# First weight block behind a norm, computed chunk by chunk of 128 tokens, in a two-layer hybrid decoder trunk

## Chip, cores and metric

The kernel runs on all 8 cores of one Trainium2 chip. Each core works on one of the 8 sequences of the batch, with no traffic between cores. The metric is the device time of the slowest core in microseconds (us).

## What is computed

Per core x is 4096 tokens by 1024 channels. Three matrix-heavy parts follow each other per layer, each behind an RMSNorm of the residual stream h; the weights are bf16 on the chip, sums are in f32.

```
for layer in (0, 1):
    y = rmsnorm(h, norm_mix_g[layer])
    if layer == 0:
        u, v, z, xBC, dt = split(y @ w_in)                  # 1024 -> 5136
        a = gelu(u) * (W_s layernorm(gelu(v)) + b)          # gMLP gating, chunks of 128
        b = rmsnorm(ssd(silu(conv(xBC)), dt) * silu(z))     # Mamba-2 scan, chunks of 128
        h = h + [a | b] @ w_out
    else:
        q, k, v = split(y @ w_qkv + b_qkv)                  # 16 heads, 2 kv heads
        h = h + window_attention(q, k, v, sinks) @ w_o + b_o
    y = rmsnorm(h, norm_mlp_g[layer])
    h = h + square(relu(y @ w_up[layer])) @ w_down[layer]   # 1024 -> 4096 -> 1024
out = rmsnorm(h, final_norm_g)
```

## The kernel before

A core takes its sequence in 8 tiles t = 0..7 of 512 tokens. A tile is 4 chunks of 128 tokens, since a norm needs tokens on the 128 partitions. `rmsnorm` (the function that yields once per chunk) does for each chunk: an ACT Square with accumulated sum (`yb<-h`), two POOL instructions for the inverse root (`small`), a DVE scalar_tensor_tensor that writes the normalized bf16 chunk (`yb<-h,small,rowb`, line 777), 8 transposes on PE (`ps<-ident_bf,yb`, line 827) into one PSUM bank, and a copy on DVE or ACT of that bank into the columns of the chunk in yTA, yTB or yT2 (`yTA<-ps`), which hold the tile with channels on partitions. From tile 4 on, the norms of rows 0, 2 and 4 (ahead of the input projection, the attention and the second MLP) transpose with a DMA and use neither PE nor PSUM; row 1 (ahead of the first MLP, called norm1) always uses PE.

The weights are cut into 51 blocks of 1024 by 512. A block lies in one of the four ring buffers `wring` and is computed by four calls of `fmajor`. Each call takes one PSUM bank and runs 8 matmuls of 512 columns into it, with 128 output channels of the block as weights and all 512 tokens of the tile as the moving side. So the first matmul of a block waits for all four chunks of the norm. Each bank is then emptied by ACT, in the MLP by a relu of 128x512 (`scr<-ps`, line 747), which DVE squares (`scr<-scr`, line 759).

PSUM has 8 banks in two pools of four, poolA and poolB, handed out in turn. The two streams that run side by side, for instance the attention of one tile and the output projection of another, have a pool each. A norm and the block behind it use the same pool.

The code only records operations with their reads and writes. A planner (`schedule`, with five passes over the recorded program, in which due times are worked out from the end) then sets one fixed order for each engine, by list scheduling over its own estimates of durations; semaphore waits are put in where an operation depends on another engine. PE works in that order: a matmul that waits holds up all that stand behind it. The reads and writes of PSUM are tracked by bank, so two matmul groups in one bank, or a group and the transposes that used the bank before, stay in the recorded order.

The record goes through the stages of the two streams with `zip_stages`. Tiles 0 and 1 go together through the first MLPs (`ups`, `dns`); from tile 2 on `mlp` does a tile at a time.

Of the kernel before, what the change touches and what calls it, by code (L numbers as in the profile page):

```python
# [8 lines left out]
AF = mybir.ActivationFunctionType  # L9
# [471 lines left out]
def _isap(x):  # L481
    return hasattr(x, "tensor") and hasattr(x, "ap")
# [3 lines left out]
PP_BQ = 80  # L486
# [20 lines left out]
PACE = 24  # L507
PST = 2
PASSES = 6
GATES = [(("w0", 0), ("x", 0, 1)), (("w0", 1), ("x", 0, 1)), (("w", 1), ("x", 1, 0)), (("w", 2), ("x", 1, 1)), (("w", 3), ("x", 1, 2)),  # L510
         *[(("x", 1, c), ("w0", 0)) for c in range(4)],
         (("gm", 0), ("w", 2)), (("gm", 1), ("w", 2)), (("ac", 0, 0), ("w", 2)), (("ac", 0, 1), ("w", 2)),
# [4 lines left out]
def build(NT=8):  # L517
    slots = due = None
    for n in range(PASSES):
        nc, st, P = record(NT, slots)  # L520
        P.due = due
        if n + 1 < PASSES:
            P.schedule()
            if n == PASSES - 3:
                due = P.backward()
            if n != PASSES - 3:
                slots = P.reslot(NW)
# [4 lines left out]
def record(NT, slots):  # L532
    nc = bass.Bass("TRN2", target_bir_lowering=False)
    st = ExitStack()
    P = Prog()
# [125 lines left out]
    qT = sview(AT, [8, 512], BF16)  # L661
# [35 lines left out]
    def nfree(ap):  # L697
        n = 1
        for s in ap.shape[1:]:
            n *= s  # L700
        return n

    def c_act(ap, accum=False):
        return 0.066 + nfree(ap) * 0.000833 + (0.12 if accum else 0.0)
# [27 lines left out]
    def ACT(out, in_, func, bias=None, scale=None, accum=None):  # L732
        kw = {}
        rd = [in_]
        wr = [out]
        if bias is not None:
            kw["bias"] = bias
            if _isap(bias):
                rd.append(bias)
        if scale is not None:  # L740
            kw["scale"] = scale
            if _isap(scale):
                rd.append(scale)
        if accum is not None:
            kw["accum_out"] = accum
            wr.append(accum)
        P.op("act", lambda e: e.activation(out=out, in_=in_, func=func, **kw), reads=rd, writes=wr,  # L747
             dur=c_act(in_, accum is not None) + 0.083 * (_isap(bias) + _isap(scale)), single=True,
             tset=TSETS.get(func))
# [39 lines left out]
    def PE(mms, extra_reads=(), writes=None):  # L789
        rd = list(extra_reads)  # L790
        wr = []
        d_ = 0.0
        l0 = mms[0][1]
        mode = 1 if l0.shape[0] == 64 else 2 if nfree(l0) == 64 else 0
        for (o, l, r, s0, s1) in mms:
            rd.append(l)
            rd.append(r)
            wr.append(o)
            d_ += c_mm(r, l)
        if writes is not None:  # L800
            wr = writes

        def fn(e, w=None):
            ins = None
            for n_, (o, l, r, s0, s1) in enumerate(mms):
                ins = e.matmul(o, lhsT=l, rhs=r, start=s0, stop=s1)  # L806
                if n_ == 0 and w is not None:
                    ins._wait_ge(w[0], w[1])
            return ins
        P.op("pe", fn, reads=rd, writes=wr, dur=d_, single="first", mode=mode)  # L810
# [44 lines left out]
    ppc = lambda c: pp[:, c:c + 1]  # L855
# [28 lines left out]
    last = NT - 1  # L884

    def wget(t, bb):
        slot = ws["free"].pop(0) if slots is None else slots[len(P.blks)][0]
        kc, cols = blocks[bb]
        n = kc * cols
        dst = wring[slot][:, 0:n]  # L890
        blk = Blk(slot)
        P.blks.append(blk)
        P.fills = blk
        store = False
        if bb not in ws["seen"]:
            nse = len(ws["seen"])
            ws["seen"].add(bb)
            if nse == 0:
                P.fills = None
                for q in range(2):  # L900
                    part = slice(q * n // 2, (q + 1) * n // 2)
                    DMA(dst[:, part], wpk_d[bb, :, part], ch_w0[q], eng="pool", issue=0.65)
                    P.mark["w0", q] = len(P.recs) - 1
                    P.early[len(P.recs) - 1] = 1e8 - 1e5 * q
                    blk.w.append(len(P.recs) - 1)
            else:
                DMA(dst, wpk_d[bb, :, 0:n], ch_ring_sw[slot], eng="pool", issue=0.65)
                if nse < 4:
                    P.early[len(P.recs) - 1] = 1e8 - 1e6 * nse
            P.mark["w", nse] = len(P.recs) - 1  # L910
            if B_WOUT <= bb < B_WOUT + 4 and (bb - B_WOUT) % 2 == 1:
                dv = dst.rearrange("p (k c) -> p k c", c=cols)
                for q in range(8):
                    TS("dve", dv[:, q, :], dv[:, q, :], ppc(PP_NG + q), ALU.mult)
            store = t < last
        else:
            DMA(dst, wscr[bb, :, 0:n], ch_ring[slot])
        P.fills = None
        if store:
            P.touch.add(blk)  # L920
            DMA(wscr[bb, :, 0:n], dst, ch_wst[slot])
            P.mark["s", len(ws["seen"]) - 1] = len(P.recs) - 1
        return Wt(P, blk, dst.rearrange("p (k c) -> p k c", c=cols))
# [73 lines left out]
    def fmajor(wv, o, yT, pool):  # L997
        bk = pool.next()
        MMG(bk, [(wv[:, k, o * 128:(o + 1) * 128], yT[:, k, :]) for k in range(8)])
        return bk  # L1000

    def tmajor(wv, tc, yT, pool):
        bk = pool.next()
        MMG(bk, [(yT[:, k, tc * 128:(tc + 1) * 128], wv[:, k, :]) for k in range(8)])
        return bk
# [115 lines left out]
            yield from z_blk(t, B, pool, wv, bi, True)  # L1121

    def u_blk(t, wv, bi, pool, fin=False):
        for o in range(4):
            P.tag = "u"
            bk = fmajor(wv, o, yd(t), pool)
            ACT(bufs(t).guT[:, 4 * bi + o, :], bk, AF.Gelu_apprx_tanh)
            if fin and o == 3:
                wdone(wv)
            yield  # L1130
# [147 lines left out]
    def ups(l, ts, fh, hp, pools):  # L1278
        yTs = [yTA, yTB]
        for b in range(0, 4, 2):  # L1280
            wvs = [wget(0, (B_UP1 if l else B_UP0) + 4 * fh + b + i) for i in range(2)]
            for t in ts:
                for i, wv in enumerate(wvs):
                    for o in range(4):
                        P.tag = "mlp%d" % l
                        bk = fmajor(wv, o, yTs[t], pools[t])
                        r = r32[o % 2]
                        ACT(r, bk, AF.Relu)
                        TT("dve", hp[:, t, 4 * (b + i) + o, :], r, r, ALU.mult)
                        if t == ts[-1] and o == 3:  # L1290
                            wdone(wv)
                        yield
# [18 lines left out]
    def mlp(t, l, yT, pool, mid=None):  # L1311
        h = hs_[t % 2]
        P.tag = "mlp%d" % l
        bu = B_UP0 if l == 0 else B_UP1
        bd = B_DN0 if l == 0 else B_DN1
        for f in range(32):
            if f % 4 == 0:
                wv = wget(t, bu + f // 4)
            bk = fmajor(wv, f % 4, yT, pool)
            r = r32[f % 2]  # L1320
            ACT(r, bk, AF.Relu)
            TT("dve", hid[:, f, :], r, r, ALU.mult)
            if f % 4 == 3:
                wdone(wv)
            yield
        yield from accum_out(t, bd, 4, lambda k: hid[:, k, :], h, pool, mid)
# [53 lines left out]

    def qkv(t, yT, pool):
        wv = wget(t, B_QKV)
        for o in range(4):
            ACT(qT[:, o, :], fmajor(wv, o, yT, pool), AF.Identity, bias=ppc(PP_BQ + o))
            yield
        wdone(wv)
        wv = wget(t, B_QKV + 2)
        bkk = fmajor(wv, 0, yT, pool)
        for kv in range(2):
            p_ = slice(64 * kv, 64 * kv + 64)  # L1390
            o_ = slice(64 - 64 * kv, 128 - 64 * kv)
            ACT(kT[p_, kv, 128:640], bkk[p_, :], AF.Identity, bias=ppc(PP_BK)[p_, :])
            DMA(kT[o_, kv, 128:640], kT[p_, kv, 128:640], ch_kt[kv])
        yield
        bk = pool.next()
        PE([(bk[:, tc * 128:(tc + 1) * 128], yT[:, k, tc * 128:(tc + 1) * 128], wv[:, k, 128:256], k == 0, k == 7)
            for tc in range(4) for k in range(8)], writes=[bk])
        TT("dve", vtok[:, 1:5, :], bk.rearrange("p (c d) -> p c d", d=128),
           bcv(BC_BV, 128).unsqueeze(1).to_broadcast([128, 4, 128]), ALU.add)
        wdone(wv)  # L1400
        yield
# [94 lines left out]
    yd = lambda t: yTB if t == 1 else yT2 if t == 2 else yTA  # L1496
# [103 lines left out]

    for a, b in GATES:
        P.recs[P.mark[a]][2].add(P.mark[b])
# [82 lines left out]
```

How the kernel before makes its waits and increments, by code:

```python
            def body(eng):  # L453
                for i in order[ename]:
                    e_, fn, deps, chan, dur, xfer = recs[i]
                    wl = list(fw[i])
                    fused = wl.pop() if (wl and self.single[i] and self.FUSE_WAIT) else None
                    for k, v in wl:
                        eng.wait_ge(sems[k], v)
                    if fused is not None and self.single[i] == "first":
                        ins = fn(eng, (sems[fused[0]], fused[1]))
                    else:
                        ins = fn(eng)
                        if fused is not None:
                            ins._wait_ge(sems[fused[0]], fused[1])
                    if chan is not None:
                        ins.then_inc(sems[chan.key], 16)
                    else:
                        ins.then_inc(sems[ename], 1)
                if ename == "sp":
                    for k, v in finals.items():
                        eng.wait_ge(sems[k], v)
# [330 lines left out]
        def fn(e, w=None):  # L803
            ins = None
            for n_, (o, l, r, s0, s1) in enumerate(mms):
                ins = e.matmul(o, lhsT=l, rhs=r, start=s0, stop=s1)
                if n_ == 0 and w is not None:
                    ins._wait_ge(w[0], w[1])
            return ins
# [14 lines left out]
        def fn(e, w=None):  # L824
# [2 lines left out]
                ins = e.transpose(out=o, in_=i_, identity=idn)  # L827
                if n_ == 0 and w is not None:
                    ins._wait_ge(w[0], w[1])
            return ins
```

The softmax here doesn't subtract the row's maximum and nothing guards it: scores larger than these inputs give would overflow.

## Time and profile before

| | |
|---|---|
| median of 3 runs | 3198.69 us (3195.86 to 3713.0) |
| profiled execution, its own time | 3202.78 us |
| its slowest core, first to last instruction | 3201.2 us (the 8 cores: 3187.0 to 3201.2) |
| PE busy | 3091.2 us, 97% of the span, 16400 matmuls |
| DVE / ACT / POOL busy | 57% / 47% / 16% |
| granted TensorE clock, mean of that core | 0.986 |

The profile is of the slowest core, number 6. Busy time counts instructions from start to end; matmuls overlap in the array, so that a busy PE is one that has a matmul under way. Idle time of an engine stands in brackets or behind a bar, with the instruction of another engine that ended it. A granted clock of 1.00 is 2.4 GHz, one of 0.5 is 1.2 GHz.

### The profile page before, as it was taken

The page shows a single profiled execution, that of the slowest core. Times are in us where ns is not written, and L with a number is a line of the kernel's source. Part 1 is how long each engine was busy: PE and PEld are TensorE (multiplying, and loading weights), DVE is VectorE, ACT ScalarE, POOL GpSimd, SP SyncE. Part 2 cuts the span into 40 slices and gives each one's busy share as a digit, 9 for nine tenths or more (in the row PEclk, how much of TensorE's full clock was granted, in tenths as well). Part 3 has the DMA queues.
Part 4 walks back from the last instruction along what each step waited for, and adds up shares of the span by engine and source line. Part 5 has one row for each costly group of instructions (what it writes and reads, how often), then busy time and mean ns, then how long its engine had stood idle before and what let it go on. Part 6 is the DMA issues. An engine that isn't in the chain of part 4 may idle for free.

```text
span 3201.2 us, 40536 instructions; the slowest of 8 cores (3187.0 to 3201.2 us)
## 1 busy us (share of the span) xinstructions
PE 3091.2 (97%) x16400; PEld 1443.9 (45%) x16400; DVE 1819.2 (57%) x2409; ACT 1497.2 (47%) x2473; POOL 503.1 (16%) x857
## 2 busy tenths in 40 slices
PE   8897999989999999999999999999999999999999
PEld 4344444434444444444544444444444444444444
DVE  5788334665454765537754486636846187454532
ACT  7775213694243644427543273624736166342421
POOL 3332101121012121001210122102210022100000
PEclk9998999999999999999999999999999999999999
DMA  9678778557757385444874469554794648637553
GB/s 201 158 161 221 167 182 203 148 157 185 178 167 228 120 251 177 147 164 139 232 236 152 145 202 235 197 165 151 222 245 153 184 145 237 211 131 201 158 182 127
DMA packets 197757, 581.42 MB, mean 182 GB/s; under 512 B 113857, under 2 KB 116673, under 8 KB 143938
## 3 DMA queue, kind: packets, MB, share of 16 engines
q1 hardware_dynamic: 190082, 525.87, 53.1%
q0 software_dynamic: 7488, 52.96, 10.5%
q8 instruction: 129, 2.11, 0.3%
q14 instruction: 58, 0.48, 0.1%
HBM read 535.00 MB, written 69.99 MB: 189 GB/s over the span
## 4 chain that ended last, share of the span: by engine, by line
PE 81%; DVE 6%; ACT 5%; DMA 5%; POOL 2%; issue 1%; SPq 0%; POOLq 0%; ACTq 0%; DVEq 0%
PE ps L806 80%; ACT scr L747 3%; DVE scr L759 3%; DMA scr<-acT 2%; DVE scr L777 1%; POOL small L759 1%; DMA wring<-wpk 1%; PE ps L827 1%; DMA h<-x 1%; ACT L747 1%; ACT yb L747 1%; POOL small L766 1%; DMA yTA<-acT 1%; DVE yb L777 1%; DVE h L759 0%
## 5 line engine op out<-in xcount | busy, mean ns | idle before, releaser
L806 PE MATMUL ps<-wring,scr 128*128 128x512 bf16 x5760 | 1275.4, 380 | 6.6 <-DVE h L759 2.2
L747 ACT ACTIVATE scr<-ps 128x512 f32<-128x512 f32 (+4 forms) x988 | 631.1, 658 | 755.0 <-PE ps L806 675.4
L806 PEld LDWEIGHTS ps<-wring,scr 128*128 128x128 bf16 x5760 | 560.5, 98 | 673.8 <-issue 18.1
L806 PE MATMUL ps<-yTA,wring 128*128 128x512 bf16 x3344 | 757.5, 381 | 3.1 <-ACT scr L747 1.8
L759 DVE TENSOR_TENSOR scr<-scr 128x512 bf16<-128x512 f32 (+2 forms) x648 | 465.7, 728 | 299.4 <-ACT scr L747 290.3
L806 PE MATMUL ps<-yTB,wring 128*128 128x512 bf16 x2672 | 615.8, 383 | 5.6 <-ACT scr L747 3.6
L759 DVE TENSOR_TENSOR h<-ps,h 128x512 f32<-128x512 f32 x288 | 197.8, 689 | 584.5 <-PE ps L806 564.4
L806 PEld LDWEIGHTS ps<-yTA,wring 128*128 128x128 bf16 x3344 | 320.9, 98 | 402.8 <-issue 32.5
L806 PEld LDWEIGHTS ps<-yTB,wring 128*128 128x128 bf16 x2672 | 259.6, 99 | 316.8 <-issue 18.0
L747 ACT ACTIVATE scr<-scr 128x256 bf16<-128x256 f32 (+4 forms) x442 | 272.1, 622 | 171.1 <-DVE scr L759 144.8
L747 ACT ACTIVATE yb<-h 128x1024 bf16<-128x1024 f32 x120 | 126.3, 1053 | 419.2 <-DVE h L759 396.0
L777 DVE SCALAR_TENSOR_TENSOR scr<-scr,pp_sb 128x512 f32<-128x512 f32 x384 | 280.0, 748 | 67.7 <-ACT scr L747 62.8
L766 POOL TENSOR_SCALAR small<-small 128x1 f32<-128x1 f32 (+1 forms) x224 | 85.0, 379 | 1425.2 <-ACT yb L747 867.5
L747 ACT ACTIVATE scr<-ps,pp_sb 128x512 f32<-128x512 f32 (+1 forms) x192 | 142.9, 747 | 123.2 <-PE ps L806 120.4
L806 PE MATMUL ps<-wring,yTA 128*128 128x512 bf16 (+1 forms) x832 | 176.7, 369 | 1.8 <-DMA wring<-wpk 0.9
L759 POOL TENSOR_TENSOR small<-small,mhalf 128x1 f32<-128x1 f32 (+1 forms) x224 | 164.4, 734 | 18.2
L747 ACT ACT_TABLE_LOAD x116 | 148.8, 1283 | 6.7 <-DVE h L768 2.6
L806 PEld LDWEIGHTS ps<-wring,yTA 128*128 128x128 bf16 x832 | 78.7, 98 | 92.8 <-issue 1.7
L759 DVE TENSOR_TENSOR scr<-scr,mask 128x1024 bf16<-128x1024 bf16 x126 | 86.4, 689 | 39.4 <-ACT scr L747 38.1
L759 DVE TENSOR_TENSOR scr<-ps,scr 128x512 bf16<-128x512 f32 (+1 forms) x96 | 82.8, 864 | 31.4 <-ACT scr L747 16.8
L759 DVE TENSOR_TENSOR scr<-scr,dts 128x1024 f32<-128x1024 f32 (+1 forms) x74 | 91.5, 1244 | 14.8 <-POOL scr L1184 9.3
L777 DVE SCALAR_TENSOR_TENSOR yb<-h,small,rowb 128x1024 bf16<-128x1024 f32 x60 | 76.9, 1282 | 38.3 <-POOL small L759 38.2
(122 smaller groups left out, 1832.2 us busy)
## 6 DMA issues: line engine op xcount, KB each, us to landing
wring<-wscr SPq DMA_DIRECT2D x320, 1024.0 KB, 5.9
wscr<-wring SPq DMA_DIRECT2D x50, 1024.0 KB, 10.5
wring<-wpk POOLq DMA_DIRECT2D x49, 1024.0 KB, 11.6
scr<-acT SPq DMA_DIRECT2D x42, 512.0 KB, 8.8
h<-x SPq DMA_DIRECT2D x36, 512.0 KB, 8.5
out<-scr SPq DMA_DIRECT2D x32, 512.0 KB, 8.2
rowb<-rows SPq DMA_DIRECT2D x28, 512.0 KB, 5.8
scr<-x SPq DMA_DIRECT2D x24, 512.0 KB, 6.6
```

The costliest lines, as they stand in the source:

```text
L747: P.op("act", lambda e: e.activation(out=out, in_=in_, func=func, **kw), reads=rd, writes=wr, dur=c_act(in_, accum is not None) + 0.083 * ...
L759: P.op(eng, lambda e: e.tensor_tensor(out=out, in0=in0, in1=in1, op=op), reads=[in0, in1], writes=[out], dur=(0.57 if nfree(out) < 16 else ...
L766: P.op(eng, lambda e: e.tensor_scalar(out=out, in0=in0, scalar1=s1, scalar2=None, op0=op0), reads=rd, writes=[out], dur=d_, single=True)
L777: P.op("dve", lambda e: e.scalar_tensor_tensor(out=out, in0=in0, scalar=scalar, in1=in1, op0=op0, op1=op1), reads=rd, writes=[out], dur=c_ ...
L806: ins = e.matmul(o, lhsT=l, rhs=r, start=s0, stop=s1)
L827: ins = e.transpose(out=o, in_=i_, identity=idn)
```

## The change

A new function `by_chunk` takes the four PSUM banks of the pool at once. It runs the same block as 16 groups of 8 matmuls of 128 columns: for each chunk c, for each quarter o of the block's output channels, the 8 matmuls of (c, o) into columns c*128 to c*128+127 of bank o. A group reads the columns of its own chunk alone. The four banks are emptied as before, each by one instruction of 512 columns, behind the group of the last chunk. It is used for 21 blocks: the first up block of both MLPs for every tile (16 blocks), the first Q block where the norm stands directly ahead of it (tiles 0, 1, 2 and 7), and the first u block of tile 3. All other blocks keep `fmajor`.

```diff
+BYC = 31
...
+    def by_chunk(wv, yT, pool):
+        bks = [pool.next() for _ in range(4)]
+        for c in range(4):
+            cs = slice(c * 128, (c + 1) * 128)
+            for o in range(4):
+                PE([(bks[o][:, cs], wv[:, k, o * 128:(o + 1) * 128], yT[:, k, cs], k == 0, k == 7) for k in range(8)],
+                   writes=[bks[o]])
+        return bks
...
     def u_blk(t, wv, bi, pool, fin=False):
+        P.tag = "u"
+        bks = by_chunk(wv, yd(t), pool) if BYC & 16 and t == 3 and bi == 0 else None
         for o in range(4):
             P.tag = "u"
-            bk = fmajor(wv, o, yd(t), pool)
+            bk = bks[o] if bks else fmajor(wv, o, yd(t), pool)
...
+                    bks = by_chunk(wv, yTs[t], pools[t]) if BYC & 8 and fh == 0 and b == 0 and i == 0 else None
...
+            if f == 0 and BYC & (1 << l):
+                bks = by_chunk(wv, yT, pool)
+            bk = bks[f] if f < 4 and BYC & (1 << l) else fmajor(wv, f % 4, yT, pool)
...
+        bks = by_chunk(wv, yT, pool) if BYC & 4 and (t <= 2 or t == last) else None
         for o in range(4):
-            ACT(qT[:, o, :], fmajor(wv, o, yT, pool), AF.Identity, bias=ppc(PP_BQ + o))
+            ACT(qT[:, o, :], bks[o] if bks else fmajor(wv, o, yT, pool), AF.Identity, bias=ppc(PP_BQ + o))
```

The planner runs on the new record, so the order of all five engines changes, also in places where the code is the same.

The order of PE at norm1 of tile 1, ahead of its first MLP. `wring,scr` are matmuls of the output projection, `ident_bf,yb` the transposes of one chunk, `yTB,wring` the up blocks; ps0 and ps1 are two banks each. Before:

```order
L806 MATMUL ps1<-wring2,scr 128x512 x8
L827 MATMUL ps0<-ident_bf,yb1 128x128 x8
L806 MATMUL ps1<-wring2,scr 128x512 x8
L827 MATMUL ps0<-ident_bf,yb0 128x128 x8
L827 MATMUL ps1<-ident_bf,yb1 128x128 x8
L827 MATMUL ps1<-ident_bf,yb0 128x128 x8
L806 MATMUL ps0<-yTB,wring1 128x512 x16
L806 MATMUL ps1<-yTB,wring1 128x512 x16
```

and with the change:

```order
L807 MATMUL ps1<-wring2,scr 128x512 x8
L828 MATMUL ps0<-ident_bf,yb1 128x128 x8
L807 MATMUL ps1<-wring2,scr 128x512 x8
L828 MATMUL ps0<-ident_bf,yb0 128x128 x8
L807 MATMUL ps0<-yTB,wring1 128x128 x32
L828 MATMUL ps1<-ident_bf,yb1 128x128 x8
L828 MATMUL ps1<-ident_bf,yb0 128x128 x8
L807 MATMUL ps1<-yTB,wring1 128x128 x24
L807 MATMUL ps0<-yTB,wring1 128x128 x16
```

Four of the 16 groups have moved between the transposes of the second and the third chunk; the other 12 stand behind those of the fourth.

The order of PE at the input norm of tile 3, ahead of its u block (`yTA,wring`), with the output projection of tile 2 beside it (`wring,scr`). Before:

```order
L827 MATMUL ps1<-ident_bf,yb0 128x128 x8
L806 MATMUL ps2<-wring3,scr 128x512 x16
L806 MATMUL ps3<-wring3,scr 128x512 x16
L806 MATMUL ps2<-wring2,scr 128x512 x16
L827 MATMUL ps1<-ident_bf,yb1 128x128 x8
L806 MATMUL ps3<-wring2,scr 128x512 x16
L827 MATMUL ps0<-ident_bf,yb0 128x128 x8
L806 MATMUL ps1<-yTA,wring0 128x512 x8
```

and with the change:

```order
L807 MATMUL ps3<-wring3,scr 128x512 x16
L807 MATMUL ps1<-yTA,wring1 128x128 x8
L807 MATMUL ps0<-yTA,wring1 128x128 x8
L807 MATMUL ps1<-yTA,wring1 128x128 x8
L807 MATMUL ps0<-yTA,wring1 128x128 x8
L807 MATMUL ps2<-wring0,scr 128x512 x16
L828 MATMUL ps1<-ident_bf,yb1 128x128 x8
L807 MATMUL ps3<-wring0,scr 128x512 x8
L807 MATMUL ps1<-yTA,wring1 128x128 x8
L828 MATMUL ps0<-ident_bf,yb0 128x128 x8
L807 MATMUL ps1<-yTA,wring1 128x128 x8
L807 MATMUL ps3<-wring0,scr 128x512 x8
```

Here four groups stand ahead of the third chunk's transposes and a fifth ahead of the fourth's, and 8 matmuls of the output projection have moved behind the fourth's.

## Rows read from the trace of the kernel before

**Rows 1.** The page: span; busy time, share and instructions of each engine.
```profile
span 3201.2 us, 40536 instructions; the slowest of 8 cores (3187.0 to 3201.2 us)
PE 3091.2 (97%) x16400; PEld 1443.9 (45%) x16400; DVE 1819.2 (57%) x2409; ACT 1497.2 (47%) x2473; POOL 503.1 (16%) x857
```

**Rows 2.** Waits of PE, whole span: total us, times, longest us.
```profile
PE ps L827 <- DVE yb L777: 27.7, 16, 5.9
PE ps L806 <- ACT scr L747: 21.7, 22, 3.1
PE ps L806 <- DVE scr L759: 20.1, 15, 4.6
PE ps L827 <- ACT scr L747: 10.9, 5, 6.4
PE ps L806 <- DMA wring<-wpk: 0.9, 1, 0.9
```

**Rows 3.** Windows view, nine norms: length, busy of five engines, clock, DMA.
```profile
255.00:278.00 23.00, 12.78 (x109) 8.96 (x110) 20.89 (x25) 12.55 (x24) 8.43 (x12) 0.68 0.99 214
342.00:358.00 16.00, 11.94 (x62) 5.86 (x61) 6.69 (x9) 7.31 (x13) 3.96 (x10) 0.79 0.31 106
990.00:1005.00 15.00, 10.46 (x41) 4.35 (x40) 4.54 (x4) 3.93 (x6) 0.79 (x2) 0.77 0.94 287
1036.00:1050.00 14.00, 10.83 (x69) 5.60 (x68) 13.28 (x20) 3.85 (x7) 2.46 (x5) 0.76 0.32 110
1248.00:1260.00 12.00, 9.77 (x63) 4.89 (x61) 7.88 (x11) 9.58 (x15) 4.26 (x7) 0.72 0.88 272
1638.00:1647.00 9.00, 5.93 (x35) 3.03 (x36) 8.04 (x12) 8.02 (x13) 3.83 (x6) 0.81 0.97 296
2028.00:2033.00 5.00, 3.71 (x30) 1.85 (x29) 3.98 (x6) 4.74 (x7) 1.22 (x2) 1.00 0.63 227
2401.00:2408.00 7.00, 3.89 (x40) 2.02 (x38) 5.83 (x9) 6.86 (x12) 3.58 (x6) 1.00 0.63 245
2779.00:2787.00 8.00, 4.63 (x46) 2.52 (x44) 6.96 (x10) 6.59 (x9) 2.74 (x4) 1.00 0.65 256
sum 109.00, PE 73.94 PEld 39.08 DVE 78.10 ACT 63.43 POOL 31.25; mean PE 8.22 PEld 4.34 DVE 8.68 ACT 7.05 POOL 3.47
```

**Rows 4.** Timeline at norm1 of tile 1: start, us, instruction, idle before.
```profile
343.02 1.06 ACT L747 ACTIVATE yb<-h 128x1024 bf16<-128x1024 f32 x1 [0.45 <-DVE h L759]
344.90 1.03 PE L827 MATMUL ps<-ident_bf,yb 128*128 128x128 bf16 x8 [2.26 <-DVE yb L777]
...
346.95 1.03 PE L827 MATMUL ps<-ident_bf,yb 128*128 128x128 bf16 x8 [1.02 <-DVE yb L777]
...
348.77 7.41 PE L806 MATMUL ps<-yTB,wring 128*128 128x512 bf16 x27 [0.79 <-DVE yTB L755]
```

**Rows 5.** Timeline of PE: runs of 128-column and of 512-column matmuls.
```profile
988.86 0.61 PE L827 MATMUL ps<-ident_bf,yb 128*128 128x128 bf16 x8
1247.41 1.95 PE L806 MATMUL ps<-wring,yTB 128*128 128x128 bf16 x32
1059.95 1.89 PE L806 MATMUL ps<-yTB,wring 128*128 128x512 bf16 x8
1787.18 13.98 PE L806 MATMUL ps<-yTA,wring 128*128 128x512 bf16 x64
```

**Rows 6.** Groups by line and form: the weight loads of the largest group.
```profile
L806 PEld LDWEIGHTS ps<-wring,scr 128*128 128x128 bf16 x5760 | 560.5, 98 | 673.8 <-issue 18.1 <-DVE h L759 3.4 <-DVE scr L759 1.6
```

**Rows 7.** Timeline: one bank of an up block emptied by ACT, squared by DVE.
```profile
352.12 0.60 ACT L747 ACTIVATE scr<-ps 128x512 f32<-128x512 f32 x1 [2.95 <-PE ps L806]
352.75 0.69 DVE L759 TENSOR_TENSOR scr<-scr 128x512 bf16<-128x512 f32 x1 [4.04 <-ACT scr L747]
```

**Rows 8.** Windows view: the first stages, where the code is unchanged.
```profile
60.00:255.00 195.00, 167.33 (x977) 83.38 (x974) 158.00 (x225) 142.87 (x239) 71.43 (x110) 0.95 0.73 168
```

More of the change, by code:

```diff
@@ L1283, in ups @@
                 for i, wv in enumerate(wvs):
+                    P.tag = "mlp%d" % l
+                    bks = by_chunk(wv, yTs[t], pools[t]) if BYC & 8 and fh == 0 and b == 0 and i == 0 else None
                     for o in range(4):
                         P.tag = "mlp%d" % l
-                        bk = fmajor(wv, o, yTs[t], pools[t])
+                        bk = bks[o] if bks else fmajor(wv, o, yTs[t], pools[t])
                         r = r32[o % 2]
@@ L1318, in mlp @@
                 wv = wget(t, bu + f // 4)
-            bk = fmajor(wv, f % 4, yT, pool)
+            if f == 0 and BYC & (1 << l):
+                bks = by_chunk(wv, yT, pool)
+            bk = bks[f] if f < 4 and BYC & (1 << l) else fmajor(wv, f % 4, yT, pool)
             r = r32[f % 2]
```

## The prediction

> **What bounds the kernel now.** I read the page first, then the waits of PE, then the stretches around the norms, then single instructions. The page says that PE has a matmul under way in 3091.2 of 3201.2 us [rows 1]; the other engines are at 57% and less. So the kernel is bound by PE nearly everywhere, and what a change can win is the 110 us in which PE is idle, and what the clock loses beside that. What it costs is any PE time that it adds. The waits of PE [rows 2] say where the idle time lies: the largest entry, 27.7 us in 16 waits, is PE in front of the transposes of a chunk that DVE has not yet normalized. That is the place of this change. The next three (21.7, 20.1 and 10.9 us) are mostly inside the scan, the attention and the setup, where the code stays as it is.
>
> The windows view [rows 3] takes the nine norms around which PE is idle for over a microsecond: norm1 of tiles 0 to 7 (at 255, 342, 1036, 1248, 1638, 2028, 2401 and 2779 us) and the input norm of tile 3 (990). Length minus PE busy is 10.2, 4.1, 4.5, 3.2, 2.2, 3.1, 1.3, 3.1 and 3.4 us, 35.1 in all (109.00 - 73.94). In the first six the granted clock is below 1. Length times (1 - clock) is the array time lost there: 7.4, 3.4, 3.5, 3.4, 3.4 and 1.7 us; of this a part lies in the idle time.
>
> What one such place looks like is in the timeline of tile 1 [rows 4]. The transposes of chunk 3 wait 2.26 us, those of chunk 4 another 1.02, and then the first up block waits 0.79 for the last copy. The transposes then take 1.03 us for 8, against 0.61 elsewhere [rows 5]: PE runs at the lower of its two levels, 1.2 GHz, after these gaps. All this time two of the four chunks lie ready in yTB and no matmul may use them.
>
> **The change, part by part.**
>
> *More matmuls.* 21 blocks of 32 matmuls of 512 columns become 21 blocks of 128 matmuls of 128 columns, 2016 more matmuls and weight loads. The pace of either comes from two runs of different length [rows 5]: 512 columns, (13.98 - 1.89) / 56 = 0.2159 us; 128 columns with new weights for each, (1.95 - 0.61) / 24 = 0.0558 us. A block goes from 32 x 0.2159 = 6.91 us to 128 x 0.0558 = 7.14 us, 0.23 us more, and 21 of them cost 4.8 us. All of it is on the path. The run of 32 is the longest of its kind in the trace, so the price of a run of 128 is bounded: below by the same columns at the 512 pace, 0.2159 / 4 = 0.054 us, which makes the cost 0; above by a weight load of 98 ns [rows 6] that overlaps nothing, 2688 x 0.098 - 21 x 6.91 = 118 us. I take 4.8, since the run of 32 is the same instruction shape.
>
> *Groups that fill the gaps.* A group (8 matmuls, one chunk and one bank) takes 8 x 0.0558 = 0.446 us. Norm and block use the same pool of four banks, and the transposes of chunk c went through the bank of output quarter c. So group (c, o) can run only when the copies of chunks c and o are both done: 1 group after the first chunk, 4 after the second, 9 after the third. The planner's order uses less than that. Ahead of the fourth chunk's transposes stand, in the nine places in order of time, 4, 4, 5 (input norm of tile 3), 4, 7, 4, 3, 4 and 4 groups. The smaller of these times 0.446 and the idle time is 1.8, 1.8, 2.2, 1.8, 2.2, 1.8, 1.3, 1.8 and 1.8, 16.5 us. Behind the fourth transposes the five groups of the first three chunks, 2.2 us, cover the last copy: 0.79 us in tile 1 [rows 4], and as much (it stands inside the 4.5) at the input norm of tile 3. Together 18.1 us. In the other 12 blocks PE has matmuls of the other stream between the chunks, or runs on through the block; there I count nothing gained, and the 0.23 us is paid all the same.
>
> *The clock.* If a gap is broken up, PE may stay at 2.4 GHz. In places 2 to 6 the loss is 3.4 + 3.5 + 3.4 + 3.4 + 1.7 = 15.4 us; between nothing and all of it I take half, 7.7 us, since about half of the idle time in these places remains. In place 1 (tile 0), where 10.2 us are idle and DVE is busy for 20.89 of 23 us, I count nothing: its chunks are late because DVE is full, not because PE waits.
>
> *Emptying four banks at once.* In `fmajor` a bank is complete every 1.73 us, ACT needs 0.60 us and DVE 0.69 [rows 7]. In `by_chunk` the four banks are complete in the last 1.8 us of the block, the first of them 1.34 us before the next block wants it. ACT's 0.60 leaves a slack of 0.74 us, less than one 1.06 us Square of a norm [rows 4]. Behind a block that waits here stands the rest of the up blocks, and beside the attention also its score matmuls. Bounds: 0, or 21 x 1.06 = 22 us. I take one block in five that meets such an instruction, 21 x 0.2 = 4.2 us, since ACT is busy 47% of the time overall and the planner places its work around this.
>
> *The moved order.* A weight block is wanted some 5 us earlier and held as much longer. PE waited 0.9 us in all for weights [rows 2], and the ring holds four blocks of 7 us each; cost 0 as long as that lead holds. The instructions of ACT, DVE and POOL and the DMAs are the same in number; SP's and POOL's queues only see them in another order. Between 60 and 255 us, ahead of the first block that changes, PE is idle for 195 - 167.3 = 27.7 us [rows 8], in waits of the setup and the first scans, and the planner has turned that order over. It can come out either way: 0, with 8 us on both sides (some 30% of that idle time).
>
> *Sum.* -18.1 - 7.7 + 4.8 + 4.2 = -16.8 us. On the profiled execution's own 3202.78 us that is 3186.0; the median of the runs is 4.1 us lower, so I predict **3182 us**.
>
> **Rivals.**
>
> *All gaps close.* The clock stays up in all places, also for half of tile 0's 7.4 us, and the banks cost nothing: -18.1 - 15.4 - 3.7 + 4.8 = -32.4, 3166 us. For it: the gaps left are short. Against it: the fill covers only half of the 35.1 us. 15%.
>
> *The gain is taken back.* The groups wait for copies that come late in their turn, PE being in order: half of the fill is lost (9 us left), the clock still falls, the banks cost 4.2 and the new order of the first scans 8: -9 + 4.8 + 4.2 + 8 = +8, 3207 us; between this and the forecast lies everything that is partly so. For it: chunk times are set by ACT, POOL and DVE (8.04 and 8.02 of 9 us busy at 1638, rows 3), which no group makes faster, and half of PE's waits are outside the norms [rows 2]. Against it: the work put in the gaps does not have to be done later. 30%.
>
> *The weight loads bind.* Each 128-column matmul brings its own weights. If a run of 128 can't keep the pace of a run of 32, and loads come at their full 98 ns [rows 6], the 21 blocks cost 118 us in place of 4.8: 3198.7 - 16.8 + 113 = 3295 us, slower by 3%. It decides from a pace of 0.0558 + 16.8 / 2688 = 0.062 us on: beyond that the change loses. Against it: the run of 32 and the transposes hold 0.056 us [rows 5], so loads of 98 ns do overlap with other loads or matmuls. 5%. The Trainium skill speaks for a milder form of it: "TensorE: Matmul & The Clock Gate", section "Back-to-back issue gap", puts a sustained stream of weight load and matmul of 128 columns at about 81 ns each. By it the 21 blocks would cost 72.6 us, and the time would be an estimated 3250 us. The trace does not agree with it for runs of 32; no run here shows one of 128.
>
> *The change does not do what it says.* If the planner put every group behind the last chunk, only its costs would be left, 3198.7 + 9 = 3208 us. It does so in 11 of the 21 blocks; in the nine places it does not, by the order. So this is part of the second rival and has no chance of its own.
>
> **How the numbers follow.** Forecast 48% (some 3172 to 3192), all gaps close 15%, taken back 30%, weight loads 5%, and 2% for what I have not seen. The range goes from 3162 (the first rival, with 4 us of luck in the order) to 3207 (the second). About one case in five lies outside, above it more than below. A measurement of this kernel tells some 2%, 64 us, from no change: faster than 3134.7 would need more than all the idle time at norms and all the clock; 1%. Slower than 3262.7 is the weight-load case with a pace above 0.085 us, or something unseen; 4%. So 95% within 2%.
>
> **What would show it.** In the profile after: runs of 128-column matmuls on `yTA,wring` and `yTB,wring` at 0.056 us each (a run of 128 lasting 7.2 us); PE's wait for `DVE yb L777` down from 27.7 to some 10 to 15 us; the clock at 1.00 in at least half of places 2 to 6; total PE idle near 90 us. A pace of 0.08, or a PE wait for `ACT scr` that grows by more than 5 us behind the new blocks, would make it wrong; so would new idle time in the first 255 us.

## The result, and the profile after

The changed kernel takes 3168.18 us (median of 4 runs, 3161.62 to 3283.05) against 3197.28 us of the kernel before (4 runs beside it). The ratio is 0.9907, with a 95% interval of 0.9882 to 0.9932: 0.93% less, some 29 us. Ratios, here and below, leave out executions in which one die ran at a lower clock than the other; medians do not. The time is inside the range given (3162 to 3207) and 14 us under the forecast, outside of the 3172 to 3192 that the forecast stands for and nearest to the first rival (3166).

The profiled execution took 3167.08 us. Its page, the span and the busy line; all line numbers behind the new function are one higher than before:

```profile
span 3165.5 us, 44543 instructions; the slowest of 8 cores (3151.6 to 3165.5 us)
PE 3082.5 (97%) x18416; PEld 1524.8 (48%) x18416; DVE 1815.3 (57%) x2409; ACT 1497.8 (47%) x2471; POOL 502.0 (16%) x857
```

Beside [rows 1] the span is 35.7 us shorter, while PE is busy for only 8.7 us less, with 2016 matmuls more. So 27.0 us are idle time that is gone (110.0 to 83.0). The waits of PE say which (total us, times, longest):

```profile
PE ps L807 <- ACT scr L748: 17.3, 18, 2.5
PE ps L828 <- DVE yb L778: 13.7, 12, 3.6
PE ps L828 <- ACT scr L748: 12.1, 4, 5.4
PE ps L807 <- DVE scr L760: 11.2, 15, 2.3
```

The wait for a normalized chunk, 27.7 us in [rows 2], is half; the waits for ACT and DVE in front of other matmuls went down too (21.7 to 17.3 and 20.1 to 11.2), and none of size has come in their place.

The windows view of the nine norms, in order of time. These stretches run from the transposes of the first chunk to the end of the first block, so they are longer than those of [rows 3]. The columns are length, busy time of PE, weight loads, DVE, ACT and POOL, then granted clock, DMA share and GB/s:

```profile
252.30:285.50 33.20, 21.46 (x269) 19.20 (x270) 27.69 (x30) 17.44 (x33) 10.27 (x16) 0.69 1.00 227
338.00:351.00 13.00, 11.09 (x169) 9.64 (x167) 6.53 (x8) 7.57 (x13) 3.78 (x9) 1.00 0.44 158
968.00:993.50 25.50, 25.22 (x237) 16.13 (x235) 10.29 (x11) 6.53 (x9) 4.05 (x7) 1.00 0.88 308
1019.00:1033.00 14.00, 12.82 (x191) 10.96 (x190) 12.90 (x21) 4.84 (x7) 2.78 (x6) 1.00 0.40 147
1228.80:1246.80 18.00, 17.73 (x229) 13.13 (x227) 11.57 (x17) 14.65 (x22) 3.48 (x8) 1.00 0.70 289
1614.00:1631.00 17.00, 17.00 (x203) 11.95 (x202) 13.62 (x21) 13.79 (x23) 4.21 (x8) 1.00 0.61 206
1994.00:2013.00 19.00, 19.00 (x213) 12.91 (x211) 14.45 (x20) 14.53 (x24) 4.38 (x8) 1.00 0.55 168
2370.00:2389.00 19.00, 19.00 (x212) 12.94 (x211) 13.93 (x19) 14.35 (x24) 3.31 (x8) 1.00 0.64 197
2743.00:2761.00 18.00, 17.09 (x225) 13.02 (x224) 12.50 (x17) 11.87 (x17) 1.84 (x5) 1.00 0.32 119
sum 176.70, PE 160.41 PEld 119.89 DVE 123.48 ACT 105.56 POOL 38.12; mean PE 17.82 PEld 13.32 DVE 13.72 ACT 11.73 POOL 4.24
```

Eight of nine are at a clock of 1.00, where five of them were below it; three have no idle time left. The first, tile 0, is the exception: 11.7 us idle and a clock of 0.69.

To make this a sum I divide the span of the slowest core in three: idle time of PE, half of PE's busy time at the 1.2 GHz level (what that level costs), and the rest, which is work at full clock.

| us, before → after | idle | cost of 1.2 GHz |
|---|---|---|
| norm1 of tile 0 | 10.2 → 11.7 | 2.0 → 6.0 |
| norm1 of tile 1 | 4.1 → 1.9 | 2.5 → 0 |
| input norm of tile 3 | 4.5 → 0.3 | 3.0 → 0 |
| norm1 of tile 2 | 3.2 → 1.2 | 3.1 → 0 |
| norm1 of tile 3 | 2.2 → 0.3 | 3.0 → 0 |
| norm1 of tile 4 | 3.4 → 0 | 1.6 → 0 |
| norm1 of tiles 5, 6, 7 | 7.8 → 0.9 | 0 → 0 |
| the nine places | 35.3 → 16.2 | 15.2 → 6.0 |
| everywhere else | 74.7 → 66.8 | 18.7 → 13.8 |

Work at full clock went from 3057.3 to 3062.7. So: -19.1 - 9.2 (nine places) - 7.9 - 4.9 (elsewhere) + 5.4 = -35.7 us.

At norm1 of tile 1 the timeline of PE (start, us, instruction, idle before) now reads as follows; the last run also holds the blocks behind the first:

```profile
340.28 0.61 PE L828 MATMUL ps<-ident_bf,yb 128*128 128x128 bf16 x8
341.82 1.96 PE L807 MATMUL ps<-yTB,wring 128*128 128x128 bf16 x32 [0.94 <-DVE yTB L756]
343.62 0.61 PE L828 MATMUL ps<-ident_bf,yb 128*128 128x128 bf16 x8
345.20 0.62 PE L828 MATMUL ps<-ident_bf,yb 128*128 128x128 bf16 x8 [0.97 <-DVE yb L778]
345.66 14.65 PE L807 MATMUL ps<-yTB,wring 128*128 128x128 bf16 x138
```

In [rows 4] PE stood 2.26, 1.02 and 0.79 us and then transposed at 1.03 us for 8. Now 32 narrow matmuls lie between the second and the third chunk, two gaps under 1 us are left, and the transposes take 0.61 and 0.62.

### The profile page after: what moved, and what is told of

Its sections match the earlier page's. It is cut to its first block, busy times and chain, and to the rows that moved or that the text cites. A ratio compares the mean times of both kernels' runs of the same rounds, so it can differ in the third digit from the quotient of the medians.

```text
span 3165.5 us, 44543 instructions; the slowest of 8 cores (3151.6 to 3165.5 us)
## 1 busy us (share of the span) xinstructions
PE 3082.5 (97%) x18416; PEld 1524.8 (48%) x18416; DVE 1815.3 (57%) x2409; ACT 1497.8 (47%) x2471; POOL 502.0 (16%) x857
## 4 chain that ended last, share of the span: by engine, by line
PE 80%; ACT 7%; DVE 6%; DMA 5%; POOL 2%; issue 1%; SPq 0%; POOLq 0%; ACTq 0%; DVEq 0%
PE ps L807 79%; ACT scr L748 4%; DVE scr L760 3%; DMA scr<-acT 3%; ACT L748 1%; PE ps L828 1%; DMA wring<-wpk 1%; POOL small L760 1%; DVE scr L778 1%; DMA h<-x 1%; POOL small L767 0%; ACT yb L748 0%; DVE yb L778 0%; DMA scr<-scr 0%; DVE h L760 0%
## 5 line engine op out<-in xcount | busy, mean ns | idle before, releaser
L748 ACT ACTIVATE scr<-ps 128x512 f32<-128x512 f32 (+5 forms) x988 | 628.8, 659 | 782.9 <-PE ps L807 651.7
L807 PEld LDWEIGHTS ps<-wring,scr 128*128 128x128 bf16 x5760 | 559.3, 98 | 667.0 <-issue 12.4
L807 PE MATMUL ps<-yTA,wring 128*128 128x512 bf16 (+1 forms) x4400 | 764.1, 329 | 3.5 <-ACT h L748 2.2
L807 PE MATMUL ps<-yTB,wring 128*128 128x512 bf16 (+1 forms) x3632 | 609.7, 323 | 7.9 <-ACT scr L748 5.4
L807 PEld LDWEIGHTS ps<-yTA,wring 128*128 128x128 bf16 x4400 | 368.2, 98 | 366.1 <-issue 32.7
L807 PEld LDWEIGHTS ps<-yTB,wring 128*128 128x128 bf16 x3632 | 299.5, 98 | 279.1 <-issue 6.9
L807 PEld LDWEIGHTS ps<-wring,yTA 128*128 128x128 bf16 x832 | 78.7, 98 | 93.4 <-issue 1.7
L760 DVE TENSOR_TENSOR scr<-scr,dts 128x1024 bf16<-128x1024 bf16 (+1 forms) x74 | 93.0, 1263 | 33.6 <-POOL scr L1196 23.6
## 6 DMA issues: line engine op xcount, KB each, us to landing
wring<-wpk POOLq DMA_DIRECT2D x49, 1024.0 KB, 11.7
```

The costliest lines, as they stand in the source:

```text
L760: P.op(eng, lambda e: e.tensor_tensor(out=out, in0=in0, in1=in1, op=op), reads=[in0, in1], writes=[out], dur=(0.57 if nfree(out) < 16 else ...
```

## Experiments

Theory A is the prediction's: groups that start before the last chunk fill the gaps, and that keeps the clock up. Theory B: the gain comes from something else that the change brings, above all the order that the planner turned over. The table holds all runs. "Ratio" is to the kernel before on the same chip; the last two columns are idle time plus cost of 1.2 GHz, as above, on the slowest core of the profiled execution (on core 5 for whole_tile_reordered and norm_in_one_bank, whose slowest cores carry the effect told in the last section, and on core 2 for without_mlp0 and core 6 for after_third_order, since some matmul records of their slowest cores are missing).

| kernel | median us | ratio [95%] | nine places | elsewhere |
|---|---|---|---|---|
| before | 3197.28 | 1 | 35.3 + 15.2 | 74.7 + 18.7 |
| before_reordered | 3202.06 | 1.0027 [1.0008, 1.0047] | 43.1 + 15.2 | 64.7 + 18.8 |
| before_third_order | 3193.44 | 1.0000 [0.9989, 1.0010] | 34.0 + 11.4 | 70.7 + 14.7 |
| whole_tile | 3183.41 | 0.9960 [0.9947, 0.9973] | 31.1 + 15.5 | 64.3 + 9.2 |
| whole_tile_reordered | 3203.04 | 1.0005 [0.9985, 1.0025] | 32.2 + 12.1 | 64.8 + 12.8 |
| changed kernel | 3168.18 | 0.9907 [0.9882, 0.9932] | 16.2 + 6.0 | 66.8 + 13.8 |
| after_reordered | 3166.97 | 0.9907 [0.9891, 0.9923] | 15.1 + 4.7 | 66.9 + 14.4 |
| after_third_order | 3160.81 | 0.9900 [0.9885, 0.9914] | 17.2 + 3.4 | 62.0 + 11.3 |
| all_up_by_chunk | 3189.11 | 0.9969 [0.9948, 0.9990] | 17.4 + 8.1 | 64.1 + 12.4 |
| norm_in_one_bank | 3180.68 | 0.9929 [0.9902, 0.9955] | 16.8 + 4.4 | 72.3 + 18.5 |
| mlp0_only | 3175.68 | 0.9942 [0.9924, 0.9959] | 21.7 + 6.7 | 70.0 + 14.3 |
| without_mlp0 | 3180.10 | 0.9937 [0.9911, 0.9963] | 26.9 + 9.7 | 64.5 + 10.7 |
| without_late_blocks | 3168.67 | 0.9918 [0.9904, 0.9932] | 17.4 + 4.0 | 72.1 + 12.8 |
| without_late_blocks_2 | 3175.54 | 0.9939 [0.9925, 0.9953] | 15.4 + 6.1 | 74.4 + 19.7 |

**whole_tile.** The same narrow matmuls, but every group waits for all four chunks:

```diff
-                   writes=[bks[o]])
+                   extra_reads=[yT[:]], writes=[bks[o]])
```

> The change with its 16 groups per block, but every group also waits for all four chunks of its tile: the 128-column shape and a new order stay, the early start is gone. Theory A (the gain is work moved into the gaps of the norms, and the clock that this keeps up): idle time of PE at the nine norms back to about 35 us, the 1.2 GHz stretches back, 5 us more for the shape: 3195 to 3210 us. Theory B (the planner's new order makes the gain, the early start is beside the point): 3160 to 3180 us, as the order here differs from that of before in as many rows as the change's does.

It took 3183.41 us, which neither theory had. Eight of the nine norms did what A says: at norm1 of tile 1 the timeline of PE is [rows 4] again, with its gaps of 2.26, about 1.1 and 0.79 us and its slow transposes,

```profile
336.53 0.91 PE L828 MATMUL ps<-ident_bf,yb 128*128 128x128 bf16 x8 [2.26 <-DVE yb L778]
338.58 1.03 PE L828 MATMUL ps<-ident_bf,yb 128*128 128x128 bf16 x8 [1.14 <-DVE yb L778]
340.40 19.80 PE L807 MATMUL ps<-yTB,wring 128*128 128x128 bf16 x179 [0.79 <-DVE yTB L756]
```

and in the windows view of tiles 1, 2 and 4 the clock is below 1 again:

```profile
336.00:356.00 20.00, 17.54 (x177) 13.23 (x178) 7.12 (x10) 7.17 (x12) 3.33 (x7) 0.83 0.31 82
1012.00:1034.00 22.00, 19.07 (x202) 14.87 (x201) 17.09 (x26) 6.42 (x10) 4.74 (x9) 0.84 0.43 144
1612.00:1635.00 23.00, 19.80 (x209) 13.02 (x208) 16.41 (x22) 14.46 (x22) 4.89 (x10) 0.93 0.62 201
```

The input norm of tile 3 is the exception. Its gap is gone here too (0.3 us idle, as in the change, against 4.5 before), and so is the lower clock:

```profile
968.00:1000.00 32.00, 31.97 (x261) 19.17 (x262) 11.19 (x14) 10.27 (x16) 3.57 (x8) 1.00 0.77 256
```

More matmuls of the output projection stand between the transposes in this order, and 8 behind those of the fourth chunk. So what the change wins at this one place is not shown to come from the early start. And outside the norms whole_tile has 73.5 us of idle time and clock cost, where the kernel before has 93.4. That asked for the same kernels in another order.

**before_reordered and after_reordered.** One constant of the planner's estimate of a matmul is changed a little; nothing that is computed changes, only the order:

```diff
-        return max(0.025, 0.0025 + n_ * 0.0004167 * f) * h_
+        return max(0.025, 0.0027 + n_ * 0.0004167 * f) * h_
```

> The kernel before, with the planner's estimate of a matmul raised by 0.2 ns: the same instructions in a slightly different order (some 100 rows of PE's 1586 stand elsewhere). Theory A: order alone is worth a few us either way: 3190 to 3204 us. Theory B: order alone can move 20 us or more: outside of that.

> The change, with the same 0.2 ns in the planner's estimate: another order of the same instructions. Theory A: the gain stays, 3160 to 3176 us, and so do the norms without 1.2 GHz in tiles 1 to 7. Theory B: the gain was one lucky order, 3176 us or more.

3202.06 and 3166.97 us: the difference between the two kernels is there in this order too, 1.2% of the time.

**whole_tile_reordered.** whole_tile with the same constant.

> The kernel in which every group waits for the whole tile, with the planner's estimate of a matmul raised by 0.2 ns. That kernel was 13 us faster than before although its norms had their gaps back: idle and clock outside of the norms had become less. If that was one lucky order (theory A), it goes towards 3195 to 3203 us here; if small groups as such give the planner better orders outside of the norms (theory C), it stays at 3178 to 3188 us.

3203.04 us, ratio 1.0005: in this order nothing is left of whole_tile's 0.4%. So that gain is not shown to come from narrow matmuls. Both versions of whole_tile (0.996 and 1.0005) have the change's matmuls and lack its early start (0.9907 twice); their order differs from the change's as well, but the nine places lie far apart: 46.6 and 44.3 us of idle time and clock cost against 22.2 and 19.8.

**before_third_order and after_third_order.** Both kernels with another slack of the planner:

```diff
-    SLACK = 0.3
+    SLACK = 0.32
```

> The kernel before in a third order (the planner's slack in front of PE 0.32 us in place of 0.30). If order alone is worth a few us: 3190 to 3205 us, with the gaps at the nine norms as before. If before was an unlucky order: clearly under 3190 us.

> The change in the same third order of the planner. If the gain belongs to the early start of the groups: 3160 to 3175 us, PE idle under 7 us at the norms of tiles 1 to 7 and the input norm, no 1.2 GHz there. If to the order: anywhere between 3165 and 3200 us.

3193.44 and 3160.81 us. Three orders of before lie at ratios of 1, 1.0027 and 1.0000, three of the change at 0.9907, 0.9907 and 0.9900. The wait for a normalized chunk (waits of PE on the slowest core; before_third_order, then after_third_order) is halved here as well:

```profile
PE ps L827 <- DVE yb L777: 27.8, 16, 7.0
```

```profile
PE ps L828 <- DVE yb L778: 13.9, 10, 4.5
```

On core 6, whose records are complete, it is 17.4 us, of which tile 0 has the most; at the norms of tiles 1 to 7 and the input norm of tile 3 PE is idle for 4.5 us, with no stretch at 1.2 GHz, as expected. 3160.81 us is the lowest median of all; its interval covers the change's own 0.9907, so it is not shown to be better.

**mlp0_only and without_mlp0.** The change for norm1 of tiles 2 to 7 alone (6 blocks), and for all but these (15 blocks):

```diff
-BYC = 31
+BYC = 1
```

```diff
-BYC = 31
+BYC = 30
```

> By chunk only in the first up block of the first MLP of tiles 2 to 7 (6 of 21 blocks, behind norm1). Theory A: idle at these six norms from 16.5 to about 2.5 us (-14), the clock there (17 us at 1.2 GHz, worth some 7 us) back, 6 blocks at 0.25 us more: -20 us, 3177 us; tile 1 and the input norm of tile 3 keep their gaps. Theory B: no relation to these norms, anywhere from 3165 to 3205 us.

> By chunk in the other 15 blocks alone; the first up block of the first MLP of tiles 2 to 7 is computed whole again. Theory A (moved work and the clock it keeps up): idle at norm1 of tiles 2 to 7 back from 2.4 to about 16.5 us, 1.2 GHz stretches back there (worth 8 us), 6 x 0.25 us saved: 3168 + 14 + 8 - 1.5 = 3188 us, while tile 1 and the input norm of tile 3 stay without gaps. Theory B (the planner's order): no such relation, 3165 to 3200 us.

3175.68 and 3180.10 us. In mlp0_only the six norms go from 16.5 to 3.8 us of idle time and from 7.7 to 0 us of clock cost; in without_mlp0 they stand as before (3.6, 2.2, 2.4, 1.3, 2.7 and 3.0 us idle), while tile 1 and the input norm of tile 3 are as in the change (1.9 and 0.3). So the effect goes with the block, place by place. The two gains, 0.58% and 0.63%, add up to 1.21%, the whole has 0.93%: equal within their intervals. A's 3188 for without_mlp0 was 8 us too slow; elsewhere this kernel has 75.2 us, against 93.4 before.

**all_up_by_chunk.** Every up block of tiles 2 to 7 is computed by chunk, 84 blocks more, where all four chunks have long been there:

```diff
-            if f == 0 and BYC & (1 << l):
+            if f % 4 == 0:
...
-            bk = bks[f] if f < 4 and BYC & (1 << l) else fmajor(wv, f % 4, yT, pool)
+            bk = bks[f % 4]
```

> By chunk in all 8 up blocks of both MLPs of tiles 2 to 7: 84 more blocks, none of them behind a norm. The price of the shape alone, 0.25 us a block: +21 us over the change, 3189 us. With the 0.2 us a block that the prediction put down for emptying four banks at once: +38 us, 3206 us, and PE waits for ACT in the MLPs. If weight loads bind in long runs: more than 3230 us.

3189.11 us, 20.9 us above the change: 0.25 us a block (from the two ratios 0.0062 ± 0.0033 of the time: 0.11 to 0.36 us). The groups of its narrow matmuls (PE's line, operands, form, count, busy us, mean ns, idle before) and its page's busy line are

```profile
L807 PE MATMUL ps<-yTA,wring 128*128 128x128 bf16 x6784 | 404.3, 220 | 0.6 <-DVE yTA L756 0.5
L807 PE MATMUL ps<-yTB,wring 128*128 128x128 bf16 x6656 | 397.9, 219 | 2.4 <-DVE yTB L756 1.7 <-ACT yTB L748 0.7
```

```profile
PE 3104.5 (97%) x26480; PEld 1870.3 (59%) x26480; DVE 1814.9 (57%) x2409; ACT 1493.8 (47%) x2475; POOL 482.4 (15%) x857
```

There are 10080 matmuls and as many loads more than in the kernel before (26480 against 16400), and in front of the 13440 narrow ones PE is idle for 3.0 us. So neither the weight loads nor the four banks that are emptied at once show a cost beside the 0.23 us of the narrower shape; the interval leaves room for 0.13 us a block.

**norm_in_one_bank.** In the change group (c, o) shares its bank with the transposes of chunk o. Here all four chunks of a norm are transposed through one bank, so that three banks are free of them:

```diff
-            b = bank16(pool.next_i())
+            if tc == 0:
+                one = pool.next_i()
+            b = bank16(one)
```

> The change, with the four transposes of a norm in one PSUM bank in place of four, so that three banks of the block are free from the start: 3, 6 and 9 groups may run after the first, second and third chunk in place of 1, 4 and 9. If the shared banks hold the fill back, the planner puts more groups ahead of the third chunk and the idle time of tiles 1 to 7 and of the input norm, 4.5 us, falls by 2 to 3 us: 3163 to 3168 us. If the transposes, which now follow each other through one bank, slow the norm instead: more idle time at the norms, 3170 to 3180 us.

3180.68 us; some of its executions carry the effect told in the last section, and the others take 3172 to 3178. With 0.9929 against the change's 0.9907 it is not better. At the nine places nothing is won (16.8 + 4.4 against 16.2 + 6.0). Instead the transposes now wait for the copy of an earlier chunk out of the same bank. The longest such wait stands at tile 0 and has no row among the change's waits; the waits of PE on cores 5 and 6:

```profile
PE ps L828 <- ACT yTA L748: 6.5, 1, 6.5
```

```profile
PE ps L828 <- ACT yTA L748: 10.2, 1, 10.2
```

At the other eight places 4.5 of the 6.0 us that are left idle on core 5 are such waits too. So freeing the banks in this way wins nothing. Whether the shared banks leave the change's remaining gaps open is not shown by it, since the one bank brings waits of its own.

**without_late_blocks and without_late_blocks_2.** The change without the second MLP's blocks of tiles 2 to 7 and without the Q blocks, where no idle time stood before: 11 blocks are left, and 10 x 0.23 = 2.3 us should be saved. The second one has the constant 0.0027 as well.

```diff
-BYC = 31
+BYC = 25
```

> By chunk only where groups came ahead of the last chunk in places with idle PE: first MLP of tiles 2 to 7, the joint MLPs of tiles 0 and 1, u of tile 3; the second MLP of tiles 2 to 7 and the Q blocks (10 blocks) are computed whole. By the price of the shape 2.5 us less than the change, 3165 us, give or take 5 us for the order; if those ten blocks did bring something: 3170 us or more.

> The same 11 blocks by chunk, in another order of the planner (a matmul's estimate 0.2 ns higher). 3160 to 3172 us if the saving of ten blocks is real and the order worth a few us.

3168.67 and 3175.54 us, the second outside what was expected. The norms keep their gain (21.4 and 21.5 us in all), and elsewhere they lose up to 13.5 us against the change (84.9 and 94.1 against 80.6). The saving of 2.3 us does not come. By the ratios to the kernel before on the same chip, the first is 0.9918 against the change's 0.9907, within the noise; the second is 0.9939 [0.9925, 0.9953] against 0.9907 [0.9891, 0.9923] for after_reordered, which has the same constant, and that is clear of it. So the ten blocks do bring something, in that order at least.

**All runs together.** At the nine places idle time and clock cost are 50.5, 58.3 and 45.4 us in the three orders of before and 46.6 and 44.3 in whole_tile's two, and 22.2, 19.8, 20.6, 25.5, 21.4 and 21.5 in the six kernels in which all these blocks start early and the norm has its own banks (the change in three orders, all_up_by_chunk and the two without late blocks): 49.0 and 21.8 in the mean, 27 us apart, with no overlap. Without tile 0 they are 27.4 to 38.3 us and 4.5 to 8.3. Theory A holds for the norms.

Everywhere else the same groups have 73.5 to 93.4 and 73.3 to 94.1 us, 82.7 and 81.8 in the mean. Theory B is right that single kernels move by up to 12 us either way there. But it is not order alone. The six kernels that compute the ten late blocks whole (three orders of before, mlp0_only and the two without late blocks) have 83.5 to 94.1 us elsewhere; the seven that compute them by chunk, with the norm's own banks, have 73.3 to 81.3, and whole_tile's two are among them. So some 10 us outside of the norms go with these ten blocks. An early start is not what it takes, since whole_tile's groups wait for the whole tile; what brings it about no run here shows.

## Why the prediction was right, and where it was off

*More matmuls: +4.8 forecast, +5.4 measured.* The timeline of PE shows 80 narrow matmuls in a row, and a whole block of 128 with 8 wide ones behind it:

```profile
2379.70 4.63 PE L807 MATMUL ps<-yTA,wring 128*128 128x128 bf16 x80
522.14 9.04 PE L807 MATMUL ps<-yTA,wring 128*128 128x128 bf16 x136
```

The first against the 8 of 0.61 us gives (4.63 - 0.61) / 72 = 0.0558 us, the pace that was taken from a run of 32 [rows 5]. The second fits too: 128 x 0.0558 + 7 x 0.2159 + 0.38 for the last = 9.03. So the rival of the weight loads is out. The Trainium skill ("TensorE: Matmul & The Clock Gate", section "Back-to-back issue gap") gives about 81 ns for such a stream. The trace does not agree: the run of 80 has 55.8 ns. By the Trainium skill's 81 ns the 84 further blocks of all_up_by_chunk would have cost an estimated 84 x (128 x 0.081 - 6.91) = 290 us; they cost 20.9.

*Groups that fill the gaps: -18.1 forecast, -19.1 measured, made up otherwise.* That the totals agree is partly luck: without tile 0 it is -20.6, against -16.3 forecast. The count of groups times 0.446 us was too low because it let nothing but groups into the gaps. At norm1 of tile 4 the timeline of PE was, before,

```profile
1637.09 0.62 PE L827 MATMUL ps<-ident_bf,yb 128*128 128x128 bf16 x8
1640.81 0.62 PE L806 MATMUL ps<-scr,vtok 128*64 128x512 bf16 x4 [3.10 <-ACT scr L747]
...
1643.15 1.03 PE L827 MATMUL ps<-ident_bf,yb 128*128 128x128 bf16 x8 [0.25 <-DVE yb L777]
1643.97 2.56 PE L806 MATMUL ps<-yTB,wring 128*128 128x512 bf16 x8
```

and is now

```profile
1617.52 0.62 PE L807 MATMUL ps<-scr,vtok 128*64 128x512 bf16 x4
...
1618.29 0.62 PE L807 MATMUL ps<-yTA,wring 128*128 128x128 bf16 x8
...
1619.16 0.62 PE L807 MATMUL ps<-yTA,wring 128*128 128x128 bf16 x8
1619.62 1.89 PE L807 MATMUL ps<-yTB,wring 128*128 128x512 bf16 x8
1621.35 0.61 PE L828 MATMUL ps<-ident_bf,yb 128*128 128x128 bf16 x8
1621.79 1.06 PE L807 MATMUL ps<-yTA,wring 128*128 128x128 bf16 x16
```

The gap waited for an exponential of the attention, which ran beside the norm. Four groups (1.8 us) stand ahead of the fourth chunk's transposes, as forecast, and with them 8 wide matmuls of the other stream (`yTB`, 1.7 us), which before stood behind these transposes. Together they cover the 3.4 us.

*Tile 0: -1.8 forecast, +1.5 by the table, nothing to speak of in fact.* Its chunks come from DVE, busy for 27.69 of 33.20 us. The timeline of PE there:

```profile
258.36 1.03 PE L828 MATMUL ps<-ident_bf,scr 128*128 128x128 bf16 x8 [5.36 <-ACT scr L748]
...
272.39 1.03 PE L828 MATMUL ps<-ident_bf,yb 128*128 128x128 bf16 x8 [3.65 <-DVE yb L778]
273.22 3.62 PE L807 MATMUL ps<-yTA,wring 128*128 128x128 bf16 x32
```

PE waits as long as before, and the first four groups run at 1.2 GHz (3.62 us, where tile 1's take 1.96). The table makes it look worse, because its two windows begin at different work. Before, the first transposes came at 259.8 us, behind a wait inside the scan that is thus not counted:

```profile
255.03 0.29 PE L806 MATMUL ps<-diagD,scr 128*128 128x128 bf16 x1 [4.63 <-DVE scr L759]
```

The change's window begins at 252.3 us and holds the 5.36 us. Over the last 40 us up to the end of the block, idle time and clock cost are 14.8 + 4.2 us before and 12.9 + 6.0 now, some 19 us both times. In the windows of the table the place has 17.7, 14.9, 16.1, 17.2, 15.5 and 15.2 us in the six kernels with early blocks in all places, 12.2 in mlp0_only, which has none here, and 12.2, 24.9 and 12.1 in the three orders of before. By the last three nothing is shown: whether tile 0 would be better off without the change is open, and a kernel with that alone was not tried.

*The clock: -7.7 forecast; the step that was mis-sized.* "Half, since half of the idle time remains" was a choice between two bounds. Of the 15.4 us, 13.2 lie in PE's busy time, and all of it is gone: no stretch at 1.2 GHz is left at any norm but tile 0's. That is -13.2 in the place of -7.7, or -9.2 with tile 0. In this the first rival was right, and the reason against it (the fill covers only half) was wrong. How much there was to win depends on the order, though: in the other two orders of before the same eight places lose 8.8 and 8.9 us, and 3.0 of the 13.2 lie at the input norm of tile 3, where whole_tile no longer has them either.

*Emptying four banks at once: +4.2 forecast, nothing found.* The wait of PE for `ACT scr` fell, and 84 blocks more cost no more than their matmuls. The chance of one in five that such a block meets a Square had no row behind it.

*The moved order: 0 ± 8 forecast, -12.8 here.* This is the largest difference from the sum. 5.6 us of it are tile 0's windows: with the last 40 us in both, it is -7.2, and the nine places have -33.9 in the place of -28.3. The kernel before has the highest value of its three orders (93.4, 83.5 and 85.4; the change: 80.6, 81.3 and 73.3). And the prediction counted nothing gained in the twelve blocks without a gap ahead of them, while in these runs some 10 us elsewhere go with the ten late ones. How much is their doing and how much is order is open: three orders of each are too few. The first 255 us, where new idle time would have spoken against the forecast, are the same: between 60 and 255 us PE is busy for 167.34 us, against 167.33 in [rows 8].

Against the -16.8 us forecast, by the windows of the table, fill, clock, banks and order came out lower by 1.0, 1.5, 4.2 and 12.8 us and the matmuls higher by 0.6: -35.7 between the profiled executions, some -29 between the medians. What was to show it did: the wait for `yb` at 13.7 us (10 to 15), the clock at 1.00 in all of places 2 to 6, idle time of 83 us (near 90). That the time lies in the range owes something to luck: clock, banks and the blocks elsewhere were all put down for too little gain or too much cost, and the range holds them only because it was carried down to the first rival.

## What to carry to other kernels

Where PE waits for the last piece of a tile, cut the first block behind it by the pieces that arrive, not by its outputs: the narrower matmuls cost 3% of one block (0.23 of 6.9 us) and what they fill is worth more than the gap itself, since the clock stays up and other work finds room between the pieces. At tile 0, where the piece is late because its producer is full, no gain shows. And where a planner sets the order, run the kernel before and the change in two or three orders: here the order alone moved one kernel by up to 0.45% (whole_tile), half as much as the change, and made an experiment without the mechanism look like a gain.

## What was not expected of the hardware

The clock came back whole where the fill was only partial. At norm1 of tile 1 PE ran at 1.2 GHz behind gaps of 2.26 and 1.02 us [rows 4]; in the change, behind two gaps of 0.94 and 0.97 us, it stays at 2.4 GHz (clock 1.00 from 338 to 351 us).

In some executions of norm_in_one_bank, whole_tile_reordered, before_reordered and the kernel before two neighbouring cores alone (0 and 1, 2 and 3, 4 and 5 or 6 and 7) have a lower clock. In norm_in_one_bank the first 255 us of core 5 and of core 6 of one execution (the windows view) are

```profile
0.00:255.00 255.00, 217.59 (x1301) 110.26 (x1301) 197.63 (x287) 192.76 (x314) 88.36 (x162) 0.95 0.77 177
```

```profile
0.00:255.00 255.00, 224.71 (x1182) 109.60 (x1205) 182.61 (x270) 182.43 (x293) 73.36 (x150) 0.85 0.74 163
```

with a clock of 0.95 and 0.85 on the same program, and core 6 ends at 3189.2 us, core 5 at 3171.4. What brings it about no run here tells.
